# FoX key tiles in pairs, values two units behind the scores, and a fourth score bank

## What is computed

```
u = RMSNorm(h);  q,k,v,z (SWA), q,k,v,z,f (FoX), gates = u @ w_in
y_swa = attend(q, [16 meta keys | window of 128], ALiBi, sinks) * silu(z)
y_fox = softmax(q k^T * scale + c_query - c_key, causal) v * silu(z)
m = sigmoid(gate_swa) * (y_swa @ w_up_swa) + sigmoid(gate_fox) * (y_fox @ w_up_fox)
h = h + RMSNorm(m @ w_out);  the meta rows are dropped
```

## Time and profile before

| | us |
|---|---|
| median of 3 runs | 812.93 (811.78 to 816.03) |
| profiled execution | 811.67 |
| its span | 809.9 |
| PE busy in the span | 789.2 (97%) |
| VectorE, ScalarE, GpSimd busy | 481.1, 315.4, 340.7 |
| granted TensorE clock | 0.999 of full |

### The profile page before, as it was taken

The page is one execution under the profiler, slowest core; times in us unless marked ns, Lnnn a source line. Parts: engine busy times, 40 slices in busy tenths (PEclk is TensorE's granted clock), DMA queues, the critical chain, the costliest instruction groups (busy, mean ns, idle before and its releaser), DMA issues.

```text
span 809.9 us, 11838 instructions
## 1 busy us (share of the span) xinstructions
PE 789.2 (97%) x4058; PEld 624.0 (77%) x4058; DVE 481.1 (59%) x1006; ACT 315.4 (39%) x650; POOL 340.7 (42%) x287
## 2 busy tenths in 40 slices
PE   6999999999999999999999999999998999999996
PEld 4998889888888888888888865655554788878885
DVE  6835258577787777645646366677777634441222
ACT  6534022343334333333334337666767122231111
POOL 1132300765445535444445325758766335512221
PEclk9999999999999999999999999999999999999999
DMA  9344114479955435344344598999800665352222
GB/s 279 107 142 112 51 41 132 135 188 246 215 141 152 111 91 152 99 122 117 99 129 121 140 280 217 232 230 232 192 1 14 224 179 157 104 207 79 104 78 79
DMA packets 127813, 116.02 MB, mean 143 GB/s; under 512 B 29693, under 2 KB 102221, under 8 KB 127754
## 3 DMA queue, kind: packets, MB, share of 16 engines
q1 hardware_dynamic: 126456, 111.53, 51.8%
q10 hardware_dynamic: 1298, 3.74, 1.2%
HBM read 81.99 MB, written 34.96 MB: 144 GB/s over the span
## 4 chain that ended last, share of the span: by engine, by line
PE 88%; issue 4%; POOL 3%; DVE 3%; ACT 2%; DVEq 0%; ACTq 0%; POOLq 0%
PE PS L1986 21%; PE PS L1987 21%; PE PS L1988 21%; PE PS L2270 4%; PE PS L2272 4%; PE PS L2271 4%; PE PS L2192 3%; PE PS L2131 2%; POOL acc L1307 2%; PE PS L2172 1%; PE PS L2207 1%; PE PS L2173 1%; PE PS L2223 1%; PE PS L2018 1%; ACT p_fox L1480 1%
## 5 line engine op out<-in xcount | busy, mean ns | idle before, releaser
L1234 POOL TENSOR_TENSOR ops<-s_sum,ops 128x512 fp32r<-128x512 f32 x64 | 91.3, 1436 | 96.7 <-ACT ops L1336 96.7
L1234 POOL TENSOR_TENSOR ops<-raw,ops 128x512 fp32r<-128x512 f32 x48 | 67.9, 1416 | 118.8 <-ACT ops L1336 118.4
L1986 PE MATMUL PS<-t_hi,ops 128*128 128x512 f32 x256 | 100.1, 391 | 0.0
L1988 PE MATMUL PS<-t_hi,ops 128*128 128x512 f32 x256 | 99.9, 390 | 0.0
L1987 PE MATMUL PS<-t_lo,ops 128*128 128x512 f32 x256 | 99.9, 390 | 0.0
L1307 POOL TENSOR_TENSOR acc<-acc,p_fox 128x400 f32<-128x400 f32 (+5 forms) x76 | 61.4, 830 | 6.9 <-ACT p_fox L1480 5.8
L1480 ACT ACTIVATE p_fox<-PS,neg_c_col 128x512 f32<-128x512 f32 (+5 forms) x112 | 54.3, 536 | 13.0 <-PE PS L2178 8.5
L1804 DVE TENSOR_TENSOR z_tmp<-u,PS 128x512 f32<-128x512 f32 x48 | 32.9, 686 | 42.7 <-PE PS L1988 23.5
L1336 ACT ACTIVATE ops<-s_sum 128x512 fp32r<-128x512 f32 x64 | 39.4, 623 | 47.9 <-DVE s_sum L1588 42.8
L1988 PEld LDWEIGHTS PS<-t_hi,ops 128*128 128x128 f32 x256 | 48.1, 188 | 10.3
L1457 ACT ACTIVATE stage_b<-z_tmp,half_bg 128x512 f32<-128x512 f32 x32 | 23.2, 725 | 82.9 <-DVE z_tmp L1804 82.9
(11 more groups left out here) (237 smaller groups left out, 2040.9 us busy)
## 6 DMA issues: line engine op xcount, KB each, us to landing
raw<-in_w_in_dram SPq DMA_DIRECT2D x34, 512.0 KB, 5.3
g_dram<-stage_b SPq DMA_DIRECT2D x32, 256.0 KB, 2.0
tanh_g<-g_dram SPq DMA_DIRECT2D x16, 512.0 KB, 4.0
x_all<-in_x_dram SPq DMA_DIRECT2D x8, 512.0 KB, 7.3
raw<-in_w_in_dram SPq DMA_DIRECT2D x16, 256.0 KB, 4.7
q_dram<-stage_b SPq DMA_DIRECT2D x16, 256.0 KB, 2.8
q_swa_dram<-stage_b SPq DMA_DIRECT2D x16, 256.0 KB, 2.9
z_dram<-stage_b SPq DMA_DIRECT2D x16, 256.0 KB, 2.0
```

What stands on the lines that cost most here:

```text
L1234: nc.gpsimd.tensor_tensor(ops[:, i % OPS, 1], op_source(p, name), ops[:, i % OPS, 0].bitcast(F32), ALU.subtract).then_inc(op_ready, 1)
L1986: pe.matmul(dst, hi_w, hi, start=first, stop=False)
L1988: return pe.matmul(dst, lo_w, hi, start=False, stop=last)
```

## The change

Narrow tiles are put in one unit with another: q = 0 has the units (0), (1, 4), (2, 3), q = 1 has (0) to (4), (5, 8), (6, 7), which makes 10 units for a pair and 40 in all. The two tiles lie side by side in one score bank and one buffer of p_fox (`unit_tiles`); each keeps its own matmuls, exponential and add. Tile 4 of q = 0 now loads 16 keys instead of 128. On PE the mask of head 0 comes right after its scores, ahead of head 1's. `S_BANKS` has a fourth bank, which was that of pv_swa; pv_swa now takes its turn in `MS_BANKS`, and the old semaphores `swa_valued` and `swa_y` become counts of that ring. The adds to acc are a step of their own, one unit behind; `values` is two units behind (`LAG`). The 32 items take units 2 to 33, one each. The tables of turns (loads, reciprocals, splits) are renumbered for 10 units, and the splits of the up weights are at four given units of pair 2.

```diff
-S_BANKS, MS_BANKS, Y_BANKS, Y_SWA_BANK = (6, 7, 4), (0, 5), (1, 2), 3
+S_BANKS, MS_BANKS, Y_BANKS = (6, 7, 4, 3), (0, 5), (1, 2)
 S_RING = len(S_BANKS)
 PT_RING = 6
+LAG = 2
 PROB_RING = 3
 FIRST_SLOT = 2
-REC_UNITS = ((4, 5, 6, 7, 8), (2, 3, 4, 5, 5))
-SECOND_LOADS = ((2, "load_queries", 0), (3, "load_keys", 0), (4, "load_values", 0), (8, "load_z", 0),
-                (9, "load_keys", 1), (10, "load_queries", 1), (11, "load_values", 1), (12, "load_z", 1))
+UNITS = (((0,), (1, 4), (2, 3)), ((0,), (1,), (2,), (3,), (4,), (5, 8), (6, 7)))
+REC_UNITS = ((4, 5, 6, 7, 7), (2, 3, 3, 4, 4))
+SECOND_LOADS = ((2, "load_queries", 0), (2, "load_keys", 0), (3, "load_values", 0), (6, "load_z", 0),
+                (7, "load_keys", 1), (8, "load_queries", 1), (9, "load_values", 1), (9, "load_z", 1))
 EARLY_UPS = 2
-SPLIT_TURNS = ((1, 0, 0, 1), (2, 1, 0, 1), (3, 2, 0, 1), (4, 3, 0, 1), (6, PAIRS + 2, 0, 2), (9, 0, 1, 2), (9, 1, 1, 2),
-               (10, 2, 1, 2), (10, 3, 1, 2), (11, PAIRS, 0, 2), (12, PAIRS + 1, 0, 2))
-NEXT_LOADS = ((1, "load_queries", None), (3, "load_keys", None), (5, "load_values", None), (6, "load_z", None))
+SPLIT_TURNS = ((1, 0, 0, 1), (2, 1, 0, 1), (2, 2, 0, 1), (3, 3, 0, 1), (4, PAIRS + 2, 0, 2), (7, 0, 1, 2), (7, 1, 1, 2),
+               (8, 2, 1, 2), (8, 3, 1, 2), (9, PAIRS, 0, 2), (9, PAIRS + 1, 0, 2))
+NEXT_LOADS = ((1, "load_queries", None), (2, "load_keys", None), (3, "load_values", None), (4, "load_z", None))
+UP_TURNS = (2, 4, 6, 8)
...
-    keys = min(P, LENGTH - P * i)
+    keys = min(P, r0 + w + N_META - P * i)
...
+def unit_tiles(q, tiles):
+
+    out, at = [], 0
+    for i in tiles:
+        r0, w, keys, masked, shift = key_tile(q, i)
+        out.append((i, at, r0, w, keys, masked, shift))
+        at += w
+    assert at <= BANK
+    return out
...
-    units = [(j, q, i) for j in range(PAIRS) for q in range(2) for i in range(4 * q + 5)]
+    units = [(j, q, tiles) for j in range(PAIRS) for q in range(2) for tiles in UNITS[q]]
     per = len(units) // PAIRS
-    spread = len(units) - 8 - FIRST_SLOT
+    spread = ITEMS
...
-        if u:
-            pj, pq, pi = units[u - 1]
-            steps.append(dict(kind="values", j=pj, q=pq, i=pi, u=u - 1, first=pi == 0, last=pi == 4 * pq + 4))
+        for kind, back in (("acc", 1), ("values", LAG)):
+            if u >= back:
+                steps.append(of_unit(kind, u - back))
...
-        if split_ups and not slot and (j >= 2):
+        if j == 2 and x in UP_TURNS:
...
-        if st["kind"] in ("score", "trans", "den"):
-            st["who"] = "dve" if st["kind"] == "score" or st["kind"] == "trans" and st["i"] % 2 else "act"
+        if st["kind"] in ("score", "trans", "den", "pv_swa"):
+            st["who"] = "dve" if st["kind"] in ("score", "pv_swa") or st["kind"] == "trans" and st["i"] % 2 else "act"
...
+                        for k, (i, at_, r0, w, keys, masked, shift) in enumerate(st["tiles"]):
+                            c0 = r0 - BANK * q
+                            dst = acc[0:keys, f % 2, h, c0:c0 + w]
+                            tile = p_fox[0:keys, n % PT_RING, at_:at_ + w]
+                            if q == 0 and i == 0:
+                                nc.gpsimd.tensor_copy(dst, tile).then_inc(acc_done["pool"], 1)
+                                continue
+                            other = p_fox[:, (n - 2) % PT_RING, :] if (q, i) == (1, 1) else dst
+                            if (n, k) in acc_before:
+                                pool.wait_ge(*acc_before[n, k])
+                            nc.gpsimd.tensor_tensor(dst, other, tile, ALU.add).then_inc(acc_done["pool"], 1)
...
-                        nc.scalar.activation(p_fox[0:keys, n % PT_RING, 0:w],
-                                             PS[0:keys, S_BANKS[n % S_RING], 0:w], ACT.Exp,
-                                             bias=neg_c_col[0:keys, i, 2 * j + h:2 * j + h + 1],
-                                             scale=1.0).then_inc(fox_exp, 1)
+                        for i, at_, r0, w, keys, masked, shift in st["tiles"]:
+                            ins = nc.scalar.activation(p_fox[0:keys, n % PT_RING, at_:at_ + w],
+                                                       PS[0:keys, S_BANKS[n % S_RING], at_:at_ + w], ACT.Exp,
+                                                       bias=neg_c_col[0:keys, i, 2 * j + h:2 * j + h + 1], scale=1.0)
+                        ins.then_inc(fox_exp, 1)
...
-                    nc.vector.scalar_tensor_tensor(out=yy, in0=PS[:, Y_SWA_BANK, :].rearrange("p (j q) -> p j q", j=PAIRS),
-                                                   scalar=0.5, in1=yy, op0=ALU.mult, op1=ALU.mult).then_inc(swa_y, 1)
-                elif kind == "values" and acc_by.get(2 * st["u"] + 1) == "dve":
-                    q, i, u = st["q"], st["i"], st["u"]
+                    items_valued(dve, t)
+                    nc.vector.scalar_tensor_tensor(out=yy, in0=PS[:, MS_BANKS[st["ms"] % 2], :].rearrange(
+                        "p (j q) -> p j q", j=PAIRS), scalar=0.5, in1=yy, op0=ALU.mult,
+                                                   op1=ALU.mult).then_inc(ms_freed["dve"], 1)
...
+                    elif u == 1:
+                        pe.wait_ge(folded, n_fold)
...
-                        dst = PS[0:keys, S_BANKS[x % S_RING], 0:w]
                         if x >= S_RING:
                             pe.wait_ge(fox_exp, x - S_RING + 1)
-                        pe.matmul(dst, KA[n][:, h, kk], QA[n][:, h, tok], start=True, stop=False)
-                        ins = pe.matmul(dst, KB[n][:, h, kk], QB[n][:, h, tok], start=False, stop=not masked)
-                        if not masked:
-                            ins.then_inc(tile_done, 1)
-                    if masked:
-                        for h in range(2):
-                            pe.matmul(PS[0:keys, S_BANKS[(2 * u + h) % S_RING], 0:masked], causal[:, 0:keys],
-                                      ident_b[:, shift:shift + masked], start=False, stop=True).then_inc(tile_done, 1)
+                        for i, at_, r0, w, keys, masked, shift in st["tiles"]:
+                            tok, kk = slice(r0, r0 + w), slice(P * i, P * i + keys)
+                            bank = PS[0:keys, S_BANKS[x % S_RING], :]
+                            dst = bank[:, at_:at_ + w]
+                            pe.matmul(dst, KA[n][:, h, kk], QA[n][:, h, tok], start=True, stop=False)
+                            ins = pe.matmul(dst, KB[n][:, h, kk], QB[n][:, h, tok], start=False, stop=not masked)
+                            if masked:
+                                ins = pe.matmul(bank[:, at_:at_ + masked], causal[:, 0:keys],
+                                                ident_b[:, shift:shift + masked], start=False, stop=True)
+                        ins.then_inc(tile_done, 1)
...
-                        ins = pe.matmul(PS[h * HEAD:(h + 1) * HEAD, Y_BANKS[f % 2], c0:c0 + w],
-                                        VF[j % 2][0:keys, i, h * HEAD:(h + 1) * HEAD],
-                                        p_fox[0:keys, x % PT_RING, 0:w], start=st["first"], stop=st["last"])
+                    for k, (i, at_, r0, w, keys, masked, shift) in enumerate(st["tiles"]):
+                        c0 = r0 - BANK * q
+                        for h in range(2):
+                            ins = pe.matmul(PS[h * HEAD:(h + 1) * HEAD, Y_BANKS[f % 2], c0:c0 + w],
+                                            VF[j % 2][0:keys, i, h * HEAD:(h + 1) * HEAD],
+                                            p_fox[0:keys, (2 * u + h) % PT_RING, at_:at_ + w], start=i == 0,
+                                            stop=st["last"] and k == len(st["tiles"]) - 1)
...
-                    else:
-                        pe.wait_ge(swa_y, t)
+                    ms_wait(pe, st["ms"])
...
-                            ins = pe.matmul(PS[g * HEAD:(g + 1) * HEAD, Y_SWA_BANK, :],
+                            ins = pe.matmul(PS[g * HEAD:(g + 1) * HEAD, MS_BANKS[st["ms"] % 2], :],
                                             v[0:w, t, g * HEAD:(g + 1) * HEAD],
                                             p_t[0:w, 2 * x + g].rearrange("p j q -> p (j q)"),
                                             start=x == 0, stop=x == 1)
-                    ins.then_inc(swa_valued, 1)
+                    ins.then_inc(ms_filled, 1)
 
```

More of the change, by code:

```diff
@@ L279, in attention_steps @@
     closing = []
[L280 to L281 removed]
+    for u, (j, q, tiles) in enumerate(units):
+        last = tiles == UNITS[q][-1]
         x = u % per
[L283 removed]
+        steps.append(dict(kind="tile", j=j, q=q, i=tiles[0], u=u, tiles=unit_tiles(q, tiles)))
         if j + 1 < PAIRS:
@@ L332, in attention_steps @@
                     steps.append(dict(kind="split_y", s=part, c0=c0, c1=c1))
-            if x == 13:
+            if x == per - 1:
                 steps.append(dict(kind="split_y", s=2 * PAIRS - 1, c0=0, c1=1))
-    j, q, i = units[-1]
```

(3 more changed lines are left out.)

83 lines of the change are left out of this document (37 added, 46 removed).

## The result

The changed kernel takes 818.5 us (median of 16 runs, 815.2 to 822.7), the kernel before beside it 812.5 (16 runs): ratio 1.007, 95% interval 1.0049 to 1.0091. I had forecast 812.9 with a range up to 817.0, so the time lies outside it, on the slow side. The profiled execution has a span of 816.9 (before 809.9). Three executions far from all others (979 us in run twelve, 1114 of the kernel before beside it, 2737 in run sixteen) are left out of every ratio, and since the last was sixteen's profiled one, its trace is not read.

A forecast was written before the change was run, and what follows sets the result against it. PE, at nine tenths or more in nearly every slice, bounds the kernel; item 16's load pins 546.8. From there 74.6 + 4.1 - 0.8 = 77.9, plus 1.9 waits, ends at 626.6: change 0.0, 812.9 us, range 808.0 to 817.0.

The forecast's parts named there:

- PE's stream: PE's work in the attention stage without waits: 140.5 us before, 139.0 after, a change of -1.5.
- the masks: Each head's mask right after its own scores on PE: 0.66 us more per pair, +2.6 us in four pairs.
- Exponential waits: PE's 4.2 us of waits for exponentials go with four score banks and values two units behind; 2.4 lie behind item 16.
- The rival that the deeper ring doesn't help: Fourth score bank: ScalarE is late, not PE early, so 2.4 us of waits stay, 815 us; chance 0.08.
- Item 16's pin: Sliding scores of item 16: their queries land near 546.7 whatever PE does, so earlier gains are lost.
- POOL and ScalarE have the same instructions as before, only bunched: Merged units on POOL and ScalarE: same instructions as before, bunched in PE's longest units; no time added.
- my 1.9: PE waits kept behind item 16, 1.9 us: denominator, and p_t copy in the last pair.
- 77.9 + 1.9: From item 16 to the first merge product: 77.9 us of PE work plus 1.9 of waits, ending at 626.6.
- The rival VectorE and the ring of two: Sliding banks behind item 16: VectorE's in-order work adds 6.3 us of waits, 819 us; slow side's chance 0.11.
- bound of 1.3 each: Sliding values in the ring of two: waits taken as 0, up to 1.3 us each if VectorE is late.
- Later loads: Pair 3's queries wait for values, later loads move by 3 to 4 us: 0 to 1.5 us slower; chance 0.1.
- The pin gives way: Item 16's queries land earlier or PE has more done: stage 6.7 to 8.7 us shorter, 804 to 806; chance 0.13.

The follow-up runs named there:

- run twelve: The kernel before the change, with only keys, values and z of pairs 2 and 3 loaded later, behind item 16's queries; 813.0 us, ratio 0.9994.
- run sixteen: The kernel of run fifteen with three score banks instead of four; 809.5 us, ratio 0.9952.
- run eight: The changed kernel with the pairing undone (one key tile in each unit) and values one unit behind the scores instead of two; 817.5 us, ratio 1.0048.
- run nine: The changed kernel with the second group of sliding queries (items 4 to 7) loaded ahead of the two z loads; 817.2 us, ratio 1.0041.
- runs two: The changed kernel with the wait for the pair before moved from query loads to value loads of pairs 2 and 3; 820.1 us, ratio 1.0080.
- run fifteen: The changed kernel with later denominators, early second sliding queries, pair 2 and 3 keys and values behind item 16's queries, gate at value loads; 809.0 us, ratio 0.9948.
- runs three: The changed kernel with only the pairing undone, one key tile in each unit; 815.9 us, ratio 1.0031.
- fourteen: The unpaired kernel of runs three with the load edits that run fifteen has; 815.6 us, ratio 1.0033.
- run one: The changed kernel with each denominator and the reciprocal, normalising and output steps behind it one unit later; 821.6 us, ratio 1.0091.
- run four: The changed kernel with values one unit behind the scores instead of two; 821.7 us, ratio 1.0101.

## Why the prediction was wrong

**PE's stream.** I said 139.0, 1.5 less than before; it is 138.65, 1.85 less, and 2.0 less by the second count. That is right. Of its parts only the masks were tested: between the heads they cost 2.8 and 3.1 us (I had 2.6).

**Exponential waits.** I dropped them, and they went. But I gave the credit to bank and distance together: run sixteen leaves the bank out and loses nothing that can be told (0.5 us), run eight puts the distance back and 1.4 us of waits for exponentials return. The rival that the deeper ring doesn't help was half right, for the ring.

**Item 16's pin.** I said 546.8 whatever PE does. It came at 545.48 and did not wait for its queries; PE was late by its own, after 1.3 and 2.9 us of waits for earlier loads that I hadn't looked for. I had read only the two items where the kernel before waited. Item 4 did not wait there, so it has no row, but merging brings it 4 us nearer to the same load (494.1 in run nine, against 498.07). The pin exists (runs two and nine wait at it), and the load edits move it.

**The step that failed** is the sentence that POOL and ScalarE have the same instructions as before, only bunched. I costed POOL at nothing, and named no work that covers it. The last unit of each half went from two adds of 0.21 to 0.28 us to two of 0.91 and two of 0.52 (the kernel before's times for these widths), 2.9 us, on the engine that PE's denominator waits for two units later, and with two normalisings queued ahead. I kept 0.65 us of denominator waits in my 1.9; they are 7.5 in the stage, 5.7 of them behind item 16. Behind item 16 the forecast was 77.9 + 1.9; measured were 87.7. The 7.9 more are 5.05 for the three denominators at 570 to 615 (5.7, of which 0.65 were in my sum) and 3.4 of half clock, less some 0.6 of other waits that didn't come.

**The clock** was in no term and no rival. It turned 4 us of waits (1.84 and 2.35) into 7.6.

**The rival VectorE and the ring of two** gave 819, the time that came, by a mechanism that wasn't there: with all else mended (run fifteen), the sliding banks that VectorE frees cost 2.4 us in three waits, the longest 1.3, inside the bound of 1.3 each that I took from the earlier trace rows. **Later loads** were seen (DMA dry near 555 to 561) and cost nothing that could be told apart: no item of the last group waited. **The pin gives way** came true only with the repairs, and in part: 809.0 measured in run fifteen, against my 804 to 806.

## What to carry to other kernels

When small pieces of work are merged, follow the largest merged piece through every engine, and ask who waits for its last result: here the cheapest tile had stood last in each half, and it was the cover of the denominator. A short group also brings forward everything timed in units, so look for loads and reused banks that did not wait before but have little room. And price a wait of about 2 us of an engine at 97% busy at its own length and, in some executions, 1.7 or 3.4 us more, since the clock may fall behind it.

## What the runs showed of the hardware

The granted clock fell to half (1.2 GHz) in this stage only at waits of 1.78 us or more in which PE had no matmul, and for 3.4 or 6.8 us, a loss of 1.7 or 3.4. In the profiles of the changed kernel and of these runs, 15 waits of 1.78 to 3.71 us were followed by it, 12 waits of 1.76 to 2.90 (2.07 in runs three and fourteen, 2.53 in run one, 2.90 in the changed kernel) were not, and none of up to 1.69 was (the 1.69 stands just ahead of the stage's first score in run four). The same kernel shows it in some executions and not in others: the changed kernel's two at 0.999 take 815.2 and 815.4 us, its thirteen at 0.991 to 0.995 take 816.8 to 822.7. The Trainium skill, "TensorE: Matmul & The Clock Gate", section "Why this matters for your kernels", tells that idle gaps between matmul bursts bring the half clock back; the traces agree, and with gaps shorter than the one it warns of too.
